# Modulation vectors of five of nine groups computed on VectorE instead of TensorE, in a hybrid S5 / gated-DeltaNet backbone

## What is computed

```python
for i in range(DEPTH):
    mx = (silu(c) @ mod_w[i] + mod_b[i]).reshape(bsz, 9, 1, 1024)
    mc = (silu(c_ctx) @ mod_w[i] + mod_b[i]).reshape(9, 1, 1, 1024)
    x  = x  + 0.5 * mx[:, 2] * swiglu(ada_norm(x,  g, mx[:, 0], mx[:, 1]), w13, w2)
    cx = cx + 0.5 * mc[2]    * swiglu(ada_norm(cx, g, mc[0],    mc[1]),    w13, w2)
    ...   # mixer with vectors 3, 4, 5; second FFN with vectors 6, 7, 8
```

## Time and profile before

| | us |
|---|---|
| median of 3 runs | 2460.81 |
| lowest and highest run | 2456.16, 2464.12 |
| the profiled execution's own time | 2459.74 |
| its span in the profile | 2457.9 |
| PE busy | 2193.1 (89%) |
| DVE busy | 1409.6 (57%) |
| ACT busy | 695.2 (28%) |
| POOL busy | 747.3 (30%) |

### The profile page before, as it was taken

The page is one execution under the profiler, slowest core; times in us unless marked ns, Lnnn a source line. Parts: engine busy times, 40 slices in busy tenths (PEclk is TensorE's granted clock), DMA queues, the critical chain, the costliest instruction groups (busy, mean ns, idle before and its releaser), DMA issues.

```text
span 2457.9 us, 34205 instructions
## 1 busy us (share of the span) xinstructions
PE 2193.1 (89%) x12846; PEld 1822.7 (74%) x12846; DVE 1409.6 (57%) x1940; ACT 695.2 (28%) x989; POOL 747.3 (30%) x588
## 2 busy tenths in 40 slices
PE   3898998964988999999899999977999999878997
PEld 0676777754876777787577778766888888868997
DVE  7866886843534433333633343547777777755555
ACT  1311221230133222212321221233433433324433
POOL 2243764733523111202320111403322332333123
PEclk7999999986689999999999999968999999988999
DMA  7354654649833343444353433211111000003553
GB/s 283 111 211 160 218 191 143 210 153 205 269 92 119 137 149 129 168 137 171 115 178 135 139 135 98 81 47 35 35 34 34 34 29 22 17 16 114 182 184 104
DMA packets 104560, 308.84 MB, mean 126 GB/s; under 512 B 27664, under 2 KB 39440, under 8 KB 95120
## 3 DMA queue, kind: packets, MB, share of 16 engines
q1 hardware_dynamic: 89248, 284.75, 34.9%
q10 hardware_dynamic: 12528, 12.33, 1.6%
q0 software_dynamic: 2688, 10.42, 1.1%
HBM read 279.21 MB, written 28.25 MB: 125 GB/s over the span
## 4 chain that ended last, share of the span: by engine, by line
PE 63%; issue 16%; DVE 8%; POOL 7%; DMA 2%; SPq 1%; ACT 1%; DVEq 1%; ACTq 0%; POOLq 0%
PE PS L205 18%; PE PS L206 17%; PE PS L207 17%; PE PS L563 2%; POOL EE L1833 2%; PE PS L1110 2%; DMA vwS<-vwd 1%; POOL DTs L1823 1%; DVE wlo L238 1%; DVE t L876 1%; POOL X L1829 1%; PE PS L1101 1%; DVE bx L877 1%; DVE bx L875 1%; DVE rstd L344 1%
## 5 line engine op out<-in xcount | busy, mean ns | idle before, releaser
L205 PE MATMUL PS<-hh,whi 128*128 128x512 f32 (+1 forms) x1792 | 665.5, 371 | 46.9 <-DVE hl L362 39.6
L207 PE MATMUL PS<-hh,wlo 128*128 128x512 f32 (+1 forms) x1792 | 653.0, 364 | 0.0
L206 PE MATMUL PS<-hl,whi 128*128 128x512 f32 (+1 forms) x1792 | 652.9, 364 | 0.0
L238 DVE TENSOR_TENSOR wlo<-raw,whi 128x1024 fp32r<-128x1024 f32 x328 | 498.5, 1560 | 91.5 <-ACT whi L232 88.3
L205 PEld LDWEIGHTS PS<-hh,whi 128*128 128x128 f32 x1792 | 341.9, 191 | 151.6 <-issue 83.7
L232 ACT ACTIVATE whi<-raw 128x1024 fp32r<-128x1024 f32 x328 | 328.9, 1051 | 314.1 <-PE PS L207 298.5
L207 PEld LDWEIGHTS PS<-hh,wlo 128*128 128x128 f32 x1792 | 342.5, 191 | 53.6
L206 PEld LDWEIGHTS PS<-hl,whi 128*128 128x128 f32 x1792 | 343.2, 191 | 48.5
L544 POOL CAST hidh<-gt 128x512 f32 (+2 forms) x88 | 54.9, 624 | 956.5 <-DVE gt L496 956.5
L205 PE MATMUL PS<-hidh,whi 128*128 128x512 f32 (+1 forms) x704 | 261.8, 372 | 29.5 <-DVE x L529 20.6
L496 DVE TENSOR_TENSOR gt<-gt,PS 128x512 f32<-128x512 f32 (+1 forms) x88 | 54.6, 620 | 397.0 <-ACT gt L471 397.0
(11 more groups left out here) (294 smaller groups left out, 2922.7 us busy)
## 6 DMA issues: line engine op xcount, KB each, us to landing
modw<-in_mod_w SPq DMA_DIRECT2D x72, 1024.0 KB, 5.2
raw<-in_w_gdn SPq DMA_DIRECT2D x32, 512.0 KB, 4.0
cxd<-cx POOLq DMA_DIRECT2D x16, 576.0 KB, 5.2
cxS<-cxd SPq DMA_DIRECT2D x8, 1152.0 KB, 6.1
raw<-in_w_f0p0a SPq DMA_DIRECT2D x16, 512.0 KB, 6.9
vwd<-vws ACTq DMA_DIRECT2D x16, 512.0 KB, 7.0
raw<-in_w_f0p1a SPq DMA_DIRECT2D x16, 512.0 KB, 6.9
raw<-in_w_glu SPq DMA_DIRECT2D x16, 512.0 KB, 4.2
```

The source lines that it names most:

```text
L205: pe.matmul(dst, w_h, xh, start=first, stop=False)
L206: pe.matmul(dst, w_h, xl, start=False, stop=False)
L207: return pe.matmul(dst, w_l, xh, start=False, stop=last)
L238: dve.tensor_tensor(wlo[:, s, c], raw[:, s, c], whi[:, s, c].bitcast(F32), ALU.subtract)\
```

## The change

Groups 4 to 8 (`PE_GROUPS = 4`) go to DVE. The host lays their weights out with the outputs on partitions: a step's 1 MB piece holds two rows of 1024 weights for each of 128 partitions. The two input vectors are broadcast over all partitions into a new tile `cb` (1 MB, loaded behind the S5 mixer, silu by ACT once). A step is now four multiply-and-add rows on DVE: two output tiles `j` by two inputs `w`, each 128x1024 with the bias as start value, and the sum goes to one column of `mods`. Each waits for the one before it. The steps stand ahead of `gate` in the up phases and ahead of the first `add_to_x` of the down blocks 0 and 1 in part (1,2). PE, ACT and POOL see no group in these parts (`g` is None), so that PE's and ACT's loops there become hardware loops.

```diff
+PE_GROUPS = 4
+def mods_where(f, p):
+    g = MODS_IN.get((f, p))
+    return g is not None and g >= PE_GROUPS
...
-        sb("spare", [P, 10496], F32, ffn)
+        cb = sb("cb", [P, 2, D], F32, ffn)
+        junk = sb("junk", [P, D], F32, ffn)
+        sb("spare", [P, 10496 - 3 * D], F32, ffn)
...
 (ffn_pe, ffn_act)
-                g, hosts = mods_after(f, p)
+                g, hosts = (None, 0) if mods_where(f, p) else mods_after(f, p)
...
 (ffn_act)
+                if (f, p) == (1, 0):
+                    act.wait_ge(cb_in, 16)
+                    act.activation(cb[:, :, :], cb[:, :, :], ACT.Silu).then_inc(cb_ready, 1)
...
                 def gate(i, s):
+                    if mods_where(f, p):
+                        mods_dve(dve, g, 2 * i + s)
                     dve.wait_ge(sil_ready[s], pairs + i + 1)
...
                 def update(i, s):
-                    if g and (i, s) == ((0, 0) if hosts == KT else (1, 0)):
+                    if mods_where(f, p):
+                        if hosts + 2 * i + s < KT:
+                            mods_dve(dve, g, hosts + 2 * i + s)
+                    elif g and (i, s) == ((0, 0) if hosts == KT else (1, 0)):
                         mods_take(dve, g)
...
+        def mods_dve(dve, g, k):
+
+            if (g, k) == (PE_GROUPS, 0):
+                dve.wait_ge(cb_ready, 1)
+            dve.wait_ge(mod_in[k % MS], 16 * ((KT * g + k) // MS + 1))
+            for j in range(2):
+                layer, a = divmod(16 * g + 2 * k + j, NMOD * KT)
+                for w in range(2):
+                    done = 4 * (KT * (g - PE_GROUPS) + k) + 2 * j + w + 1
+                    dve.tensor_tensor_reduce(out=junk[:, :], in0=modw[:, k % MS, D * j:D * j + D], in1=cb[:, w, :], scale=1.0,
+                                             scalar=modb[:, layer, a:a + 1], op0=ALU.mult, op1=ALU.add,
+                                             accum_out=mods[:, layer, a, w:w + 1]).then_inc(vector_done, 1)
+                    dve.wait_ge(vector_done, done)
+            dve.sem_inc(mod_used[k % MS], 1)
+            if k == KT - 1:
+                dve.sem_inc(mods_ready, 1)
+                mods_derived(dve, g)
...
 (load_both, on SP's queue)
                 for j in range(COUNT[name]):
+                    if name == "f1p0a" and j == 2:
+                        for q in range(2):
+                            sp.wait_ge(x_ready[q], 1 + X_BEFORE[2])
+                        sp.dma_start(cb[:, :, :], A["cb"]).then_inc(cb_in, 16)
                     load_halves(sp, name, j % 2, (BASE[name] + j) // 2, A["w_" + name][j])
...
 (layout, on the host)
+    rows = I["mod_w"].transpose(0, 2, 1).reshape(2 * NMOD * KT // 2, 2, P, D).transpose(0, 2, 1, 3).reshape(-1, P, 2 * D)
+    a["mod_w"] = np.concatenate([a["mod_w"][:PE_GROUPS * KT], rows[PE_GROUPS * KT:]])
+    a["cb"] = np.broadcast_to(np.stack([I["c_ctx"].reshape(D), I["c"][0].reshape(D)]), (P, 2, D))
```

More of the change, by code:

```diff
@@ L178, in program @@
         mod_turned = sem("mod_turned")
+        cb_in = sem("cb_in")
+        cb_ready = sem("cb_ready")
+        vector_done = sem("vector_done")
         silu_c = sem("silu_c")
@@ L500, in update @@
                 def update(i, s):
-                    if g and (i, s) == ((0, 0) if hosts == KT else (1, 0)):
+                    if mods_where(f, p):
+                        if hosts + 2 * i + s < KT:
+                            mods_dve(dve, g, hosts + 2 * i + s)
+                    elif g and (i, s) == ((0, 0) if hosts == KT else (1, 0)):
                         mods_take(dve, g)
-                        if p == 0:
-                            dve.wait_ge(mods_ready, mods_done(layer, n_, 2))
+                    if p == 0 and g and (i, s) == (0, 0):
+                        dve.wait_ge(mods_ready, mods_done(layer, n_, 2))
                     dve.wait_ge(acc_even, KT // 2 * (len(PARTS) * f + p) + 2 * i + s + 1)
@@ L589, in mods_take, with mods_derived @@
             dve.wait_ge(mods_ready, (MODS_DONE[g - 1] if g else 1) + 1)
+            mods_derived(dve, g)
+        def mods_derived(dve, g):
+            vector = mods[:, :, :, :].rearrange("p l a w -> p (l a) w")[:, 16 * g:16 * g + 16, :]
             for h_ in range(2):
```

## The result

The changed kernel takes 2416.27 us (median of 4 runs, 2413.34 to 2419.88) against 2458.48 us before (median of 4, 2455.71 to 2464.12): a ratio of 0.983, 95% interval 0.981 to 0.985, 42 us less. The forecast was 2414 us. The profiled execution took 2417.77 us, its span is 2416.0 us, 41.9 us shorter than that of before.

A forecast was written before the change was run, and what follows sets the result against it. PE's queue was taken to bound FFN 1 and FFN 2. 52.2 us leaving PE less 6.8 given back in part (1,2) made -45.4 us from 2459.74, so 2414 us, range 2407 to 2422.

The forecast's parts named there:

- The bound: In FFN 1 and FFN 2 PE's queue is the path, busy 397 of 406 us and 388 of 400 us.
- What leaves PE: In FFN 1 and 2, forty steps at 1.22 us and five turns leave PE's path: 52.2 us.
- The turns: Five groups' turns in down blocks leave PE, 0.67 us each by ACT's waits, 3.4 us together.
- The loops cost nothing: PE's and ACT's loops becoming hardware loops costs nothing, since 10.88 us a block was measured in such a loop.
- T: Distance from one new DVE multiply-and-add row to the next, write-out included: taken as 1.4 us.
- The high end: Upper bound for a DVE row, if the running sum is paced like the scan: 2.3 to 2.4 us with write-out.
- the low end: Lower bound for a DVE row, 1.24 us; the value was taken near it, assuming one addition per element.
- The room: In an up block DVE has 6.1 us idle between split and gate; four rows take 5.6 us and fit.
- What part (1,2) gives back: At its down blocks PE waits for hid 1.2 us, x 2.6 and 2.0, plus POOL 1: 6.8 us lost.
- DVE as the bound: Rival: DVE's rows at 2.3 us pace FFN 1 and 2, giving 2534 us; decides from 1.84 us; chance 0.12.
- The in-between rival: Rival: DVE rows take 1.6 to 1.8 us by dearer write-out or wait on itself; 2446 us; chance 0.08.
- wait elsewhere: Rival: PE meets new waits of 2 to 4 us at each of five phases' ends or starts; 2424 to 2430 us; chance 0.10.

The follow-up runs named there:

- the short rows: The changed kernel with DVE's rows 64 instead of 1024 elements long, so the sums leave out most terms: 2407.45 us.
- the repeated profile: The changed kernel itself, unaltered, measured and profiled again on the same chip as a later run: 2416.93 us.
- The runs with five and six rows: The changed kernel with five or six DVE rows in each step instead of four, some computed again: 2447.09 us and 2498.61 us.
- the rows behind the additions: The changed kernel with steps 6 and 7 in part (1,2) placed behind the additions to x instead of ahead: 2416.62 us.

## Why the prediction was right, and where it was off

**The bound** was read rightly: PE's queue is the path in both FFNs, and DVE was idle there.

**What leaves PE.** Forecast 52.2 us. The steps gave 1.22 us each, as read from silu's distances. The turns were sized too low: 0.67 us from ACT's idle time, but in that block ACT had also copied the rows out, so that its idle time understates the block. The distances themselves give 0.95: from the last silu of (1,0) to the split that the end of the first down block releases it was 13.06 us before, against 12.11 in a block with a step alone. 5 x 0.95 instead of 5 x 0.67 makes 53.6 us, and the eight-block parts gained 10.6 to 10.8 us instead of 10.4.

**"The loops cost nothing"** was the one step that failed. It is true of PE. The row on which it rested is of a part whose loop is entered with the right table in place; part (2,0), behind a norm, was not, and cost 1.6 us. The mechanism needs two things, a late silu and a DVE without room, as the short rows show.

**T** was forecast at 1.4 and is 1.33. The pointer scalar and the undisturbed 1.23 us gave 1.28 for the row, measured 1.285; the write-out is 0.083 us rather than 0.15 and overlaps. The high end, from the scan's two steps for each element, did not come: 1.04 ns per element is what a plain operation takes as well, (1230 - 684) / 512 = 1.07 ns. The choice of the low end rested on a reading that no row showed; this run bears it out. The Trainium skill's rule ("Vector Engine (DVE) Microarchitecture Reference", section 7, half rate for a scalar-tensor-tensor form with two SBUF sources that are not bf16, for lack of a read port for the accumulator) does not hold for this instruction, which takes two float32 sources from SBUF and writes its sum out: 1.285 us for 1024 elements, where twice 1.04 ns for each element would be above 2.1. The trace names it as a custom instruction and not as the scalar-tensor-tensor form of that rule, so whether the rule is meant for it stays open. Another of its rules agrees: "VectorE: DVE Perf Modes", section "Two Vector instructions with no wait between them", counts an operation that writes its accumulator as two instructions, and the trace shows both.

**The room** was forecast at 6.1 us for 5.6 us of rows; measured, once the lag of (1,0) is gone, DVE still waits 0.8 to 1.0 us for silu at a gate in FFN 1, and 0.3 to 0.4 at the last gate of (1,0) and (1,1), behind the derived vectors. The lag at the start of (1,0) and its recovery came as described, and the new silu cost nothing: norm to first silu 23.76 us against 23.67.

**What part (1,2) gives back** was forecast at 6.8 us: two waits of 2.6 and 2.0, one of 1.2 for `hidl`, and 1 for POOL. The two waits are 2.25 and 3.17 us, the second longer by a row that took 2.31 us beside POOL's sum of the squares; that for `hidl` is 1.0. What was left out is the clock: 1.7 us at half speed behind the second wait. In the repeated profile it fell behind the first wait instead, where the second wait covers it, and the part was 1.6 us shorter (last section). The term was right in its mechanism and some 2 us too small.

**The rivals.** DVE as the bound was put at T = 1.84 as the turning point. The runs with five and six rows have an effective T of 1.66 and 2.0 and lie on the two sides, 16 us under and 36 us over before. For T = 2.0 the prediction's own formula gives 32 x (0.58 + 0.48 + 2 x 0.38) = 58 and 24 x 0.38 + 8 x 0.6 = 14 on top of -45, +26 to +27; the measured +36 is 9 more; the matmuls slowed behind the waits account for about that much (12.8 us of delay in the two FFNs against 2.5 after). So the turning point is lower than 1.84; a straight line between the two runs puts it near 1.77, an estimate. The in-between rival (T of 1.6 to 1.8) did not happen. Nor did the "wait elsewhere" (its own terms, five times 2 to 4 us, reach 2434 and not 2430): the ends of (1,0), (1,1) and (2,1) cost 0.1 us each, and only that of (2,0), where ACT's table loads make silu late, has a wait for `hidl`, of 1.23 us.

**The sum**: forecast -45.4 against 2459.74; measured -43.4 in the two FFNs and -41.9 over the whole span, the rest being the scatter ahead of FFN 1. That the FFNs come so close is in part luck: the turns gave 1.4 us more than forecast, and (2,0) gave back 1.6 and (1,2) 1.9 that were not in the sum.

## What to carry to other kernels

Work that is moved off the bounding engine is free as long as each period of the receiving engine has room for it; compare capacity per block, not the busy share over the whole kernel, and place the work where the blocks are long (here the down blocks of 10.88 us rather than those of 8.16). Where an engine missed its period here, another order inside the block did not help, and moving the work to longer blocks did. Before a written-out loop on ACT is made a hardware loop, ask which function table is in place at its entry, since in (2,0) the reload landed in every pass.

## What the runs showed of the hardware

A wait of PE can cost more than its length. After 3.17 us of idle the granted clock was 0.57 over 4 us (+1.7 us); after 7.25 us of idle it was 0.50 for 4 us and 0.86 for 4 more, and in the run with five rows this made up about 9 of 28 us. Which wait has a drop behind it is not fixed by its length: the one of 2.25 us in the changed kernel has none, those of 2.84 and 2.33 us with the rows behind the additions have one each. Where the drop falls matters as much. In the changed kernel's repeated profile the two waits of (1,2) again end 11.6 us apart, and the clock fell behind the first one, of 2.24 us. PE then came to the second, which DVE ends, 1.65 us later in relation to it, waited 1.52 us instead of 3.17, and ran at the full clock behind it. Its windows (length, busy time and instructions of PE, PEld, DVE, ACT and POOL, granted clock, DMA share, GB/s):

```profile
1144.00:1148.00 4.00, 3.24 (x10) 2.56 (x11) 4.00 (x6) 0.65 (x1) 3.14 (x3) 0.77 0.03 8
1148.00:1152.00 4.00, 4.00 (x16) 3.23 (x15) 3.96 (x4) 0.00 (x0) 2.02 (x1) 0.80 0.73 225
...
1156.00:1160.00 4.00, 3.63 (x16) 2.98 (x17) 4.00 (x5) 0.98 (x2) 3.19 (x2) 1.00 0.13 35
```

The same half clock cost 1.7 us behind the last wait of the part, and nothing where another engine ended the next wait.

Where instructions of DVE and POOL overlap, they delay one another. A row of 1.285 us takes 2.31 us when it meets POOL's `hidl` (2.05 us), and POOL's copy `hidh` takes 1.43 us instead of 0.61 at the first block of (1,0), as its timeline shows, after and before:

```profile
821.91 1.43 POOL L566 CAST hidh<-gt 128x512 f32 x1 [36.52 <-DVE gt L515]
823.51 2.05 POOL L568 TENSOR_TENSOR hidl<-gt,hidh 128x512 f32 x1 [0.17 <-POOL hidh L566]
```

```profile
815.85 0.61 POOL L544 CAST hidh<-gt 128x512 f32 x1 [32.83 <-DVE gt L496]
816.64 2.04 POOL L546 TENSOR_TENSOR hidl<-gt,hidh 128x512 f32 x1 [0.17 <-POOL hidh L544]
```

When DVE's order shifted, the cost moved from one instruction to another (the split was shorter by 1.06 us, the row longer by 1.03) and the block's sum stayed.
